# The end of a decoder step rearranged: low parts, projection, norms and gates

## Chip, cores and metric

One NeuronCore of a Trainium2 chip runs the whole program. The metric is the device time of one execution in microseconds (us). PE is TensorE, DVE VectorE, ACT ScalarE, POOL GpSimd, SP SyncE.

## What is computed

One decoder layer on 576 tokens (512 of a prompt, 64 of eight samples) with 2048 channels. The change touches what follows the expert (PEER) block:

```
x = x + peer(rms_norm(x, ln2))
x = x + sigmoid(rms_norm(x, ln_ple) @ w_ple_gate) * (p @ w_ple_proj)
y = rms_norm(x, ln_final)          # rms_norm(x,g) = x * rsqrt(mean(x*x)+eps) * g
```

## The kernel before

Activations lie feature-major in SBUF: `x` is 16 tiles (KD) of 128 channels by 576 tokens (T). Products are made in about fp32 by three matmuls of rounded operands: high times high, high times low and low times high. So each weight block of 128x1024 (512 KB) is loaded by SP (`loads`, `value_load`), rounded by ACT to `whi`, and its low part `raw - whi` is made by DVE or POOL (`split`, `value_low`; "lowering" below). There are two buffers for ordinary blocks and four in the value phase. Each engine runs its own program in order and waits on semaphores.

**Value phase** (DVE's `values`, L1530 to L1560; PE matmuls at L2085). 32 groups of 8 blocks, two output tiles a block. PE multiplies the expert activations `a_hi`, `a_lo` (416 tokens) with the value blocks; DVE adds each PSUM tile to `x`, lowers blocks, makes the next group's activations (`product` L1497, `low` L1505; ACT's `a_hi` between them), and does five `axpy` (L1530) a group for the other 160 tokens, for which POOL gathers one element (`pick`, L575) and one row of 8 KB a partition (`row`, L583) for each. Of every four value blocks POOL lowers the third (L591): blocks 2, 6, 10 and so on. PE starts group g when all four activations of the group are lowered (`a_rdy`). At the phase's start POOL does, in order: wait, lower block 2, two memsets, 10 picks, 5 rows, then rows and picks of the next groups, each row waiting for the `axpy` that frees its buffer, with block 6 lowered after two of these.

**End.** PE transposes the gathered sums (L2100, L2104) and DVE adds them to `x` (nine adds; semaphore `gx`). DVE lowers two blocks and `p` (`hi_lo`), and PE makes the 16 tiles of `p @ w_ple_proj` (2x2 K-blocks, 12 matmuls a tile, four tiles a weight block); DVE copies each to `proj` (L1594). Then `norm(2)`: ACT squares a tile, PE sums it over the channels by a matmul with ones (L1658), the two in turns for 16 tiles; DVE and ACT form the root (`rms_m`, Sqrt, reciprocal and a Newton step, L978 to L984); DVE scales, ACT rounds, DVE lowers each of 16 tiles `h`. Then 16 gate tiles, 96 matmuls each, two weight blocks each: ACT takes the sigmoid out of PSUM, DVE multiplies with `proj` and adds to `x`. Then `norm(3)`, again 16 squares and sums after the last gate, the root, 16 scalings (L1022), and 8 DMAs of `y`.

Of the kernel before, what the change touches and what calls it, by code (L numbers as in the profile page):

```python
# [19 lines left out]
F32 = mybir.dt.float32  # L20
# [6 lines left out]
P = 128  # L27
# [125 lines left out]
def build(nc, d, o):  # L153
    ctx = ExitStack()
    with ctx:
# [126 lines left out]
        def v_slot(b):  # L282
# [4 lines left out]
        (p_hi, p_lo, proj, sg), _ = run(rM, ("p_hi", [P, 2, T], F32R), ("p_lo", [P, 2, T], F32R),  # L287
                                        ("proj", [P, KD, T], F32), ("sg", [P, 2, T], F32))
        p_raw = at("p_raw", [P, 2, T], F32, rZ + 4 * TB)
# [5 lines left out]
        def ring_b(t):  # L295
# [12 lines left out]
            a_sel axpy gx_t gx""".split()  # L308
# [7 lines left out]
        def _(sp):  # L316
# [71 lines left out]
            for n in range(KD // 2):  # L388
                sp.wait_ge(S["h_done"], 3 * KD + 2 * n + 2)
                sp.dma_start(o["y"][:, 2 * n:2 * n + 2], x[:, 2 * n:2 * n + 2]).then_inc(S["out"], 16)  # L390
# [11 lines left out]
        def _(pool):  # L402
# [191 lines left out]
            for u in range(2):  # L594
                pool.wait_ge(S[f"asp{u}"], 16 * (PRE // 2))
            pool.wait_ge(s_used, B_PG)
            pool.wait_ge(S["v_hi"], 3)
# [3 lines left out]
            for n in range(2 * GR_X):  # L601
                pick(n)
            pool.wait_ge(S["relaid"], 32 * NV)
            for n in range(GR_X):
                row(n)
            for g in range(NG):
                for i in range(GR_X):
# [4 lines left out]
                    if i == 1:  # L612
                        value_low(8 * g + 6)
# [3 lines left out]
            pool.wait_ge(S["gat"], NCHUNK)  # L617
            pool.dma_start(p_raw[:], d["pT"]).then_inc(S["p"], 16)
# [3 lines left out]
        def _(act):  # L622
# [314 lines left out]
            weights(B_PG + 2, 2)  # L937
            act.wait_ge(S["v_free"], 2 * NV)
            act.wait_ge(S["gx"], 9)
            norm(2)  # L940
            with act.Fori(0, KD // 2 - 1) as i:
                for u in range(2):
                    split(B_PG + 6 + 2 * u, [(i, 4)])
                    split(B_PG + 7 + 2 * u, [(i, 4)])

                    act.wait_ge(S["pas"], i * 2 + (u + 1))
                    nc.scalar.activation(halves(sg[:, u]), ring_b(u), ACT.Sigmoid).then_inc(s_free_b, 1)
            for n in (KD - 2, KD - 1):
                if n == KD - 2:
                    split(N_BLOCKS - 2)  # L950
                    split(N_BLOCKS - 1)
                act.wait_ge(s_used, B_PG + 4 + 2 * n + 2)
                act.wait_ge(S["pas"], n + 1)
                nc.scalar.activation(halves(sg[:, n % 2]), ring_b(n), ACT.Sigmoid).then_inc(s_free_b, 1)
            act.wait_ge(S["pas"], KD + 2)
            norm(3)
# [3 lines left out]
        def _(dve):  # L960
# [572 lines left out]
            def values(g, loops=(), more=True):  # L1533
# [3 lines left out]
                turns = (0, 1, 2, 4, 5) if not more else (3, 4, 5, 6, 7) if g == 0 else (1, 2, 3, 6, 7)  # L1537
# [4 lines left out]
                for j in range(8):  # L1542
# [12 lines left out]
                    if j in turns:  # L1555
                        axpy(g, turns.index(j), loops)

# [5 lines left out]
            values(0)  # L1563
            with dve.Fori(0, (NG - 2) // 2) as i:
# [5 lines left out]

            for q in range(4):
                dve.wait_ge(S["gx_t"], q + 1)
                src = PS[:, 4 + q, :].rearrange("p (f t) -> p f t", f=4)
                for c, t0 in ((slice(64, P), NP_TOK - 64), (slice(0, 64), NP_TOK)):
                    xt = x[:, 4 * q:4 * q + 4, t0:t0 + 64]
                    v.tensor_tensor(xt, xt, src[:, :, c], ALU.add).then_inc(S["gx"], 1)
            dve.wait_ge(S["gx_t"], 5)
            xt = x[:, :, TD:TD + TX]
            v.tensor_tensor(xt, xt, PS[:, 0, :].rearrange("p (f t) -> p f t", f=KD), ALU.add).then_inc(S["gx"], 1)
            dve.wait_ge(S["gx"], 9)  # L1580
            for u in range(2):
                split(B_PG + u)

            dve.wait_ge(S["p"], 16)
            for k in range(2):
                hi_lo(p_raw[:, k], p_hi[:, k], p_lo[:, k]).then_inc(S["p_done"], 1)
            for q in range(4):
                for m in range(4):
                    if m < 3:
# [650 lines left out]
```

## Time and profile before

| | us |
|---|---|
| median of 3 runs | 5093.37 |
| lowest, highest | 5090.38, 5096.75 |
| profiled execution, its own time | 5095.67 |
| its span in the trace | 5094.1 |

| busy in the span | us | share |
|---|---|---|
| PE | 4956.0 | 97% |
| DVE | 2410.8 | 47% |
| ACT | 1284.1 | 25% |
| POOL | 1413.1 | 28% |

The granted clock over the span is 0.984 of full speed. The shares are means over very different phases. The value phase lies at 3571 to 4760 us, the end at 4760 to 5094 us; there the views by window and the timelines of the engines are to be read.

### The profile page before, as it was taken

The numbers are of one execution on the slowest core, as the hardware profiler recorded it, in microseconds if no ns is written. First come the engines' busy times: TensorE is split into PE (matmuls) and PEld (weight loads), VectorE is DVE, ScalarE is ACT, GpSimd is POOL, SyncE is SP. The second block draws the span as 40 slices with busy tenths as digits, with TensorE's granted clock in tenths as the row PEclk, the third lists the DMA queues.
The fourth block names the chain that finished last, engine by engine and source line by source line (L and its number), as shares of the span: only waits on it lengthen the run. The fifth ranks groups of instructions, "written<-read, shape, count | busy, mean of one in ns | idle before, by whom it ended". The sixth has DMA issues, their size and how long they took to land.

```text
span 5094.1 us, 86630 instructions
## 1 busy us (share of the span) xinstructions
PE 4956.0 (97%) x34109; PEld 4834.1 (95%) x34109; DVE 2410.8 (47%) x4330; ACT 1284.1 (25%) x1701; POOL 1413.1 (28%) x928
## 2 busy tenths in 40 slices
PE   8999999999998999999999999999899999999897
PEld 7999999989997999999999999999899999999797
DVE  4333442234325789122222100000799999999633
ACT  3113332123212112222222222222222222222232
POOL 1000000010000024333333344444555555555000
PEclk9999999899999999999999999999999999999999
DMA  5553345455543443244445443333888889888222
GB/s 171 156 161 115 122 149 167 132 156 167 178 122 92 147 146 106 95 162 164 159 160 179 164 147 110 106 106 132 292 308 301 309 301 309 299 303 295 89 74 78
DMA packets 505376, 882.44 MB, mean 173 GB/s; under 512 B 34016, under 2 KB 365808, under 8 KB 482432
## 3 DMA queue, kind: packets, MB, share of 16 engines
q1 hardware_dynamic: 184128, 468.24, 27.9%
q0 software_dynamic: 50784, 278.14, 14.6%
q10 hardware_dynamic: 270336, 134.25, 9.5%
q8 instruction: 92, 1.51, 0.1%
q14 instruction: 36, 0.29, 0.0%
HBM read 796.23 MB, written 220.46 MB: 200 GB/s over the span
## 4 chain that ended last, share of the span: by engine, by line
PE 82%; DVE 9%; issue 6%; ACT 1%; POOL 1%; DMA 1%; DVEq 0%; ACTq 0%; SPq 0%; POOLq 0%
PE PS L1634 65%; PE PS L2085 10%; PE PS L2057 2%; DVE v_lo L1512 2%; DVE x L1546 1%; PE PS L1658 1%; DVE acc L1530 1%; ACT w_hi L902 1%; DVE a_lo L1505 1%; DVE af L1497 1%; DVE h_lo L1002 1%; DVE w_lo L1512 0%; PE PS L1748 0%; PE PS L2003 0%; PE PS L1686 0%
## 5 line engine op out<-in xcount | busy, mean ns | idle before, releaser
L1634 PE MATMUL PS<-h_hi,w_hi 128*128 128x288 f32 x7808 | 1714.9, 301 | 50.6 <-DVE h_lo L1002 41.0
L1634 PE MATMUL PS<-h_hi,w_lo 128*128 128x288 f32 x7808 | 1681.0, 297 | 0.0
L1634 PE MATMUL PS<-h_lo,w_hi 128*128 128x288 f32 x7808 | 1679.6, 297 | 0.0
L1634 PEld LDWEIGHTS PS<-h_hi,w_hi 128*128 128x128 f32 x7808 | 1262.8, 190 | 91.3 <-issue 63.5
L1634 PEld LDWEIGHTS PS<-h_lo,w_hi 128*128 128x128 f32 x7808 | 1265.8, 190 | 0.0
L1634 PEld LDWEIGHTS PS<-h_hi,w_lo 128*128 128x128 f32 x7808 | 1265.5, 190 | 0.0
L628 ACT ACTIVATE w_hi<-w_raw 128x1024 fp32r<-128x1024 f32 x522 | 553.2, 1060 | 2326.2 <-PE PS L1634 2295.0
L537 POOL TENSOR_TENSOR w_lo<-w_raw,w_hi 128x1024 fp32r<-128x1024 f32 x254 | 619.8, 2440 | 1528.6 <-ACT w_hi L628 1528.5
L967 DVE TENSOR_TENSOR w_lo<-w_raw,w_hi 128x1024 fp32r<-128x1024 f32 x270 | 330.2, 1224 | 662.3 <-ACT w_hi L628 646.8
L2085 PE MATMUL PS<-a_hi,v_hi 128*128 128x416 f32 x1024 | 362.4, 354 | 19.2 <-POOL v_lo L591 19.1
L1472 DVE TENSOR_SCALAR oh_j<-iota,oh_cur 128x128 f32<-128x128 f32 x416 | 117.4, 282 | 542.7 <-PE PS L2057 542.5
L2085 PE MATMUL PS<-a_hi,v_lo 128*128 128x416 f32 x1024 | 362.6, 354 | 0.0
L2085 PE MATMUL PS<-a_hi,w_lo 128*128 128x416 f32 x1024 | 361.5, 353 | 0.0
L2085 PE MATMUL PS<-a_lo,v_hi 128*128 128x416 f32 x1024 | 359.0, 351 | 0.0
L2085 PE MATMUL PS<-a_hi,w_hi 128*128 128x416 f32 x1024 | 358.8, 350 | 0.0
L2085 PE MATMUL PS<-a_lo,w_hi 128*128 128x416 f32 x1024 | 357.4, 349 | 0.0
L1497 DVE TENSOR_TENSOR af<-gl,g_in 128x416 f32<-128x416 f32 x128 | 81.1, 634 | 567.8 <-DMA g_in<-gate_scr 567.8
L583 POOL DMA_INDIRECT rows<-v_rows,row_i x160 | 202.2, 1264 | 471.5 <-DVE acc L1530 443.3
L1530 DVE SCALAR_TENSOR_TENSOR acc<-rows,a_sel,acc 128x2048 f32<-128x2048 f32 x128 | 300.3, 2346 | 8.6 <-issue 8.6
L575 POOL DMA_INDIRECT a_el<-act_scr,act_i x160 | 276.1, 1726 | 48.6 <-issue 48.6
L1546 DVE TENSOR_TENSOR x<-x,PS 128x416 f32<-128x416 f32 x512 | 277.7, 580 | 18.8 <-PE PS L2085 16.1
L892 ACT ACTIVATE a_hi<-af 128x416 fp32r<-128x416 f32 x128 | 70.7, 552 | 764.9 <-DVE af L1497 647.3
(288 smaller groups left out, 5080.0 us busy)
## 6 DMA issues: line engine op xcount, KB each, us to landing
w_raw<-in_w SPq DMA_DIRECT2D x652, 512.0 KB, 3.9
v_rows<-in_w ACTq DMA_DIRECT2D x512, 256.0 KB, 3.8
v_raw<-in_w SPq DMA_DIRECT2D x128, 512.0 KB
act_scr<-gsp POOLq DMA_DIRECT2D x128, 288.0 KB, 3.6
gate_scr<-g_st POOLq DMA_DIRECT2D x13, 2048.0 KB, 8.8
gl<-act_scr SPq DMA_DIRECT2D x32, 832.0 KB
g_in<-gate_scr SPq DMA_DIRECT2D x32, 832.0 KB
spill_scr<-spill POOLq DMA_DIRECT2D x40, 288.0 KB, 4.6
```

The source lines that it names most:

```text
L537: nc.gpsimd.tensor_tensor(wlo[:, b % 2], raw[:, b % 2], whi[:, b % 2].bitcast(F32), ALU.subtract).then_inc(s_lo, 1)
L575: pool.indirect_dma_start(a_el[:, n:n + 1], None, act_flat, bass.IndirectOffsetOnAxis(ap=act_i[:, n // GR_X, n % GR_X].unsqueeze(1), axis= ...
L583: pool.indirect_dma_start(rows[:, n % GR_X], None, v_rows, bass.IndirectOffsetOnAxis(ap=row_i[:, n // GR_X, n % GR_X].unsqueeze(1), axis=0 ...
L628: nc.scalar.activation(whi[:, b % 2], raw[:, b % 2], ACT.Copy).then_inc(s_hi, 1)
L967: v.tensor_tensor(wlo[:, b % 2], raw[:, b % 2], whi[:, b % 2].bitcast(F32), ALU.subtract).then_inc(s_lo, 1)
L1472: ch.did(v.tensor_scalar(oh_j[:, n % 2, k], iota[:], cur[:, 2:3], None, ALU.is_equal))
L1497: v.tensor_tensor(af[:, c % 2].rearrange("p (b t) -> p b t", b=ND), gl[:, par, k].rearrange("p (b t) -> p b t", b=ND), g_in[:, par, :, k], ...
L1512: v.tensor_tensor(q[2], q[0], q[1].bitcast(F32), ALU.subtract).then_inc(S["v_lo"], 1)
L1530: v.scalar_tensor_tensor(dst[:], rows[:, i], a_sel[:, bass.ds(at_step(n, kl), 1)], dst[:], ALU.mult, ALU.add).then_inc(S["axpy"], 1)
L1546: v.tensor_tensor(xt, xt, PS[:, (2 * j + m) % 8, 0:TD], ALU.add).then_inc(S["v_free"], 1)
L1634: ins = mm(dst[:, a], w[:, m, at + n], xx[:, k, a * TH:(a + 1) * TH], start=first and n == 0 and r == 0, stop=last and n == len(ks) - 1 an ...
L2085: ins = mm(PS[:, f % 8, 0:TD], w[:, m, k], xx[:, par, k], start=k + r == 0, stop=k == GRP - 1 and r == 2)
```

## The change

At the start of the value phase POOL lowers block 2 before it waits for stored activations, and block 6 after 5 picks and 5 rows; the other 5 picks follow. `p` is loaded there, and DVE takes it apart, and lowers the first two projection blocks, in the last value group, whose five `axpy` are drawn together to its steps 0 to 4.

PE transposes each quarter as soon as its tiles are free, and starts the projection's first tile before `gx` is complete. ACT meanwhile rounds `x * lns` (without the root) to `h_hi`, and squares each tile; POOL adds the squares into `ss`; PE sums only this one tile over the channels (`summed`). DVE makes the low parts between its copies (`low_part`). The factor `rstd2` is multiplied in when a gate tile leaves PSUM (DVE), and ACT's sigmoid then works in SBUF. In the gate phase ACT squares each finished `x` tile and multiplies it by `lns`, and POOL adds 14 of the 16 squares. After the last gate, PE sums `ss` and the last square, and the root and 16 plain multiplications follow. Indentation is cut by eight and unchanged lines are left out in part:

```diff
@@ -284,9 +284,13 @@
     return (raw[:, q], whi[:, q], wlo[:, q]) if q < 2 else (raw2[:, q - 2], whi2[:, q - 2], wlo2[:, q - 2])
-(p_hi, p_lo, proj, sg), _ = run(rM, ("p_hi", [P, 2, T], F32R), ("p_lo", [P, 2, T], F32R),
-                                ("proj", [P, KD, T], F32), ("sg", [P, 2, T], F32))
-p_raw = at("p_raw", [P, 2, T], F32, rZ + 4 * TB)
+(proj, sg, rms2, rstd2), _ = run(rM, ("proj", [P, KD, T], F32), ("sg", [P, 2, T], F32),
+                                 ("rms2", [P, T], F32), ("rstd2", [P, T], F32))
+p_hi = at("p_hi", [P, 2, T], F32R, rZ + 4 * TB)
+assert rZ + 7 * TB <= rE
+p_raw, p_lo = at("p_raw", [P, 2, T], F32, rR), at("p_lo", [P, 2, T], F32R, rR)
+sq4 = at("sq4", [P, 4, T], F32, rZ)
+ss = at("ss", [P, T], F32, rZ + 6 * TB)
 PS = ctx.enter_context(nc.psum_tensor("PS", [P, 8, 512], F32))
 def ring_a(t):
...
@@ -386,7 +390,7 @@
     loads(B_PG + 2, N_BLOCKS, SKIP)
     for n in range(KD // 2):
-        sp.wait_ge(S["h_done"], 3 * KD + 2 * n + 2)
+        sp.wait_ge(S["yd"], 2 * n + 2)
         sp.dma_start(o["y"][:, 2 * n:2 * n + 2], x[:, 2 * n:2 * n + 2]).then_inc(S["out"], 16)
     sp.wait_ge(S["out"], 16 * (KD // 2))
@@ -591,31 +595,43 @@
         nc.gpsimd.tensor_tensor(q[2], q[0], q[1].bitcast(F32), ALU.subtract).then_inc(S["v_lop"], 1)
     pool.wait_ge(S["index"], 1)
-    for u in range(2):
-        pool.wait_ge(S[f"asp{u}"], 16 * (PRE // 2))
     pool.wait_ge(s_used, B_PG)
-    pool.wait_ge(S["v_hi"], 3)
     value_low(2)
     nc.gpsimd.memset(acc_x[:], 0.0).then_inc(S["axpy"], 1)
-    for n in range(2 * GR_X):
+    for u in range(2):
+        pool.wait_ge(S[f"asp{u}"], 16 * (PRE // 2))
+    for n in range(GR_X):
         pick(n)
+    pool.dma_start(p_raw[:], d["pT"]).then_inc(S["p"], 16)
     pool.wait_ge(S["relaid"], 32 * NV)
         row(n)
+    value_low(6)
+    for n in range(GR_X, 2 * GR_X):
+        pick(n)
     for g in range(NG):
                 pick(GR_X * (g + 2) + i)
-            if i == 1:
+            if i == 1 and g:
                 value_low(8 * g + 6)
                 value_low(8 * g + 10)
-    pool.wait_ge(S["gat"], NCHUNK)
-    pool.dma_start(p_raw[:], d["pT"]).then_inc(S["p"], 16)
+    def add_square(r, k):
+        i = (KD - 1) * (r - 2) + k
+        pool.wait_ge(S["sqd"], KD * (r - 2) + k + 1)
+        pool.wait_ge(S["ssq"], i - 1)
+        nc.gpsimd.tensor_tensor(ss[:], ss[:], sq4[:, k % 4], ALU.add).then_inc(S["ssq"], 1)
+    for k in range(1, KD):
+        add_square(2, k)
+    for k in range(1, KD - 1):
+        add_square(3, k)
 @block.scalar
@@ -934,26 +950,52 @@
         nc.scalar.activation(whi[:, u], raw[:, u], ACT.Copy).then_inc(s_hi, 1)
-    weights(B_PG + 2, 2)
-    act.wait_ge(S["v_free"], 2 * NV)
-    act.wait_ge(S["gx"], 9)
-    norm(2)
-    with act.Fori(0, KD // 2 - 1) as i:
-        for u in range(2):
-            split(B_PG + 6 + 2 * u, [(i, 4)])
-            split(B_PG + 7 + 2 * u, [(i, 4)])
-            act.wait_ge(S["pas"], i * 2 + (u + 1))
-            nc.scalar.activation(halves(sg[:, u]), ring_b(u), ACT.Sigmoid).then_inc(s_free_b, 1)
-    for n in (KD - 2, KD - 1):
-        if n == KD - 2:
-            split(N_BLOCKS - 2)
-            split(N_BLOCKS - 1)
-        act.wait_ge(s_used, B_PG + 4 + 2 * n + 2)
-        act.wait_ge(S["pas"], n + 1)
-        nc.scalar.activation(halves(sg[:, n % 2]), ring_b(n), ACT.Sigmoid).then_inc(s_free_b, 1)
-    act.wait_ge(S["pas"], KD + 2)
-    norm(3)
+    def square(r, k):
+        if k == 0:
+            if r > 2:
+                act.wait_ge(S["summed"], r - 2)
+            dst = ss[:]
+        else:
+            if r > 2 or k > 4:
+                act.wait_ge(S["ssq"], (KD - 1) * (r - 2) + max(k - 4, 0))
+            dst = sq4[:, k % 4]
+        nc.scalar.activation(dst, x[:, k], ACT.Square).then_inc(S["sqd"], 1)
+    for k in range(KD):
+        if k == 0:
+            act.wait_ge(S["gx"], 9)
+        nc.scalar.activation(h_hi[:, k], x[:, k], ACT.Copy, scale=lns[:, 2, k:k + 1]).then_inc(S["hh2"], 1)
+        square(2, k)
+        if k in (4, 8, 12, 15):
+            split(B_PG + 1 + (k + 1) // 4)
+    split(B_PG + 6)
+    split(B_PG + 7)
+    act.wait_ge(S["ms"], 3)
+    nc.scalar.activation(rstd2[:], rms2[:], ACT.Sqrt).then_inc(S["rt"], 1)
+    def sigmoid(t):
+        act.wait_ge(s_free_b, N_SPILL + NCHUNK + t + 1)
+        nc.scalar.activation(sg[:, t % 2], sg[:, t % 2], ACT.Sigmoid).then_inc(S["sgm"], 1)
+    def squared_and_weighed(t):
+        act.wait_ge(S["pas"], t + 1)
+        square(3, t)
+        act.wait_ge(S["sqd"], KD + t + 1)
+        nc.scalar.activation(x[:, t], x[:, t], ACT.Copy, scale=lns[:, 3, t:t + 1]).then_inc(S["xl"], 1)
+    for t in range(KD):
+        if 0 < t < KD - 1:
+            split(B_PG + 6 + 2 * t)
+            split(B_PG + 7 + 2 * t)
+        sigmoid(t)
+        if t == KD - 1:
+            nc.scalar.activation(tok[:], part[:], ACT.Sqrt).then_inc(S["rt"], 1)
+        else:
+            squared_and_weighed(t)
+    squared_and_weighed(KD - 1)
+    act.wait_ge(S["ms"], 4)
+    nc.scalar.activation(rstd2[:], rms2[:], ACT.Sqrt).then_inc(S["rt"], 1)
 @block.vector
@@ -1534,7 +1576,7 @@
         bl = [(r, 8 * n) for r, n in loops]
         fl = [(r, KD * n) for r, n in loops]
-        turns = (0, 1, 2, 4, 5) if not more else (3, 4, 5, 6, 7) if g == 0 else (1, 2, 3, 6, 7)
+        turns = (0, 1, 2, 3, 4) if not more else (3, 4, 5, 6, 7) if g == 0 else (1, 2, 3, 6, 7)
         if g:
@@ -1554,6 +1596,12 @@
                 axpy(g, turns.index(j), loops)
+            if not more and j >= 5:
+                if j == 5:
+                    for q in range(2):
+                        hi_lo(p_raw[:, q], p_hi[:, q], p_lo[:, q]).then_inc(S["p_done"], 1)
+                else:
+                    split(B_PG + j - 6)
     for c in range(GRP):
@@ -1561,60 +1609,85 @@
     values(0)
+    dve.wait_ge(S["p"], 16)
     with dve.Fori(0, (NG - 2) // 2) as i:
     dve.wait_ge(S["v_free"], 2 * NV)
-    for q in range(4):
+    def gathered(q):
         dve.wait_ge(S["gx_t"], q + 1)
             v.tensor_tensor(xt, xt, src[:, :, c], ALU.add).then_inc(S["gx"], 1)
+    def projected(n):
+        q, m = n // 4, n % 4
+        if m < 3:
+            dve.wait_ge(S["vt"], NV + 3 * q + m + 1)
+        else:
+            dve.wait_ge(s_used, B_PG + q + 1)
+        v.tensor_copy(halves(proj[:, n]), ring_a(n)).then_inc(s_free_a, 1)
+    def low_part(k):
+        dve.wait_ge(S["hh2"], k + 1)
+        v.scalar_tensor_tensor(h_lo[:, k], x[:, k], lns[:, 2, k:k + 1], h_hi[:, k].bitcast(F32), ALU.mult,
+                               ALU.subtract).then_inc(S["h_done"], 1)
+    def root(r):
+        dve.wait_ge(S["summed"], r - 1)
+        v.tensor_scalar(halves(rms2[:]), PS[:, 0:2, 0:TH], 1.0 / D, EPS, ALU.mult, ALU.add
+                        ).then_inc(S["ms"], 1)
+        if r == 2:
+            split(B_PG + 7)
+        dve.wait_ge(S["rt"], 3 if r == 2 else 5)
+        inverse_root(rstd2, rms2)
+    for q in range(4):
+        gathered(q)
     dve.wait_ge(S["gx_t"], 5)
     xt = x[:, :, TD:TD + TX]
-    v.tensor_tensor(xt, xt, PS[:, 0, :].rearrange("p (f t) -> p f t", f=KD), ALU.add).then_inc(S["gx"], 1)
+    v.tensor_tensor(xt, xt, PS[:, 3, :].rearrange("p (f t) -> p f t", f=KD), ALU.add).then_inc(S["gx"], 1)
     dve.wait_ge(S["gx"], 9)
-    for u in range(2):
-        split(B_PG + u)
-    dve.wait_ge(S["p"], 16)
-    for k in range(2):
-        hi_lo(p_raw[:, k], p_hi[:, k], p_lo[:, k]).then_inc(S["p_done"], 1)
-    for q in range(4):
-        for m in range(4):
-            if m < 3:
-                dve.wait_ge(S["vt"], NV + 3 * q + m + 1)
-            else:
-                dve.wait_ge(s_used, B_PG + q + 1)
-                split(B_PG + q + 2)
-            v.tensor_copy(halves(proj[:, 4 * q + m]), ring_a(m)).then_inc(s_free_a, 1)
-    dve.wait_ge(s_free_a, A_PG + KD)
-    norm(2, True)
-    dve.sem_inc(S["pas"], 2)
+    for n in range(KD):
+        projected(n)
+        if n >= 3 and n % 2 == 1:
+            low_part((n - 3) // 2)
+        if n in (5, 9, 13):
+            split(B_PG + 2 + n // 4 - 1)
+    for k in range(7, KD):
+        low_part(k)
+        if k == 10:
+            split(B_PG + 5)
+    split(B_PG + 6)
+    root(2)
     def ple(t, loops=(), more=True):
         bl, tl = [(r, 4) for r in loops], [(r, 2) for r in loops]
+        more = more and (t > 0 or loops)
         if more:
-            split(B_PG + 4 + 2 * t + 2, bl)
-            split(B_PG + 4 + 2 * t + 3, bl)
-        dve.wait_ge(s_free_b, at_step(N_SPILL + NCHUNK + t + 1, tl))
+            split(B_PG + 6 + 2 * t, bl)
+        dve.wait_ge(s_used, at_step(B_PG + 6 + 2 * t, bl))
+        v.tensor_tensor(halves(sg[:, t % 2]), ring_b(t), halves(rstd2[:]), ALU.mult).then_inc(s_free_b, 1)
+        if more:
+            split(B_PG + 7 + 2 * t, bl)
+        dve.wait_ge(S["sgm"], at_step(t + 1, tl))
         n = at_step(t, tl)
         v.tensor_tensor(x[:, n], x[:, n], proj[:, n], ALU.add).then_inc(S["pas"], 1)
+    ple(0)
     with ch.loop(KD // 2 - 1, 2) as i:
         for u in range(2):
-            ple(u, [i])
-    ple(KD - 2)
+            ple(1 + u, [i])
     ple(KD - 1, more=False)
-    dve.wait_ge(S["pas"], KD + 2)
-    norm(3, False)
+    root(3)
+    for k in range(KD):
+        dve.wait_ge(S["xl"], k + 1)
+        v.tensor_tensor(x[:, k], x[:, k], rstd2[:], ALU.mult).then_inc(S["yd"], 1)
 @block.tensor
@@ -2094,28 +2167,45 @@
     pe.wait_ge(S["axpy"], NK_G + 2)
-    pe.wait_ge(S["v_free"], 2 * NV)
     for q in range(4):
+        pe.wait_ge(S["v_free"], 2 * NV - 3 + q)
         for f in range(4):
     for f in range(KD):
-        ins = mm(PS[:, 0, f * TX:(f + 1) * TX], acc_x[:, f * P:(f + 1) * P], sel_x[:], start=True, stop=True)
+        ins = mm(PS[:, 3, f * TX:(f + 1) * TX], acc_x[:, f * P:(f + 1) * P], sel_x[:], start=True, stop=True)
     ins.then_inc(S["gx_t"], 1)
-    pe.wait_ge(S["gx"], 9)
+    def summed(src, first=True, last=True):
+        for a in range(2):
+            ins = mm(PS[:, a, 0:TH], ones[:], src[:, a * TH:(a + 1) * TH], start=first, stop=last)
+        if last:
+            ins.then_inc(S["summed"], 1)
     pe.wait_ge(S["p_done"], 2)
             pe.wait_ge(s_free_a, A_PG + 4 * q + m - 1)
+            if q == 0 and m == 1:
+                pe.wait_ge(S["gx"], 9)
             tile(ring_a(m), None, (q % 2, m, 2), p_hi, p_lo, range(2), True, True
                  ).then_inc(S["vt"] if m < 3 else s_used, 1)
-    norm(2)
-    project(ring_b, s_free_b, N_SPILL + NCHUNK, 2 * KD, B_PG + 4, KD)
-    norm(3)
+    full_tile(ring_b(0), B_PG + 4, h_hi, h_lo, h0=2 * KD)
+    pe.wait_ge(s_free_a, A_PG + KD)
+    pe.wait_ge(S["ssq"], KD - 1)
+    summed(ss[:])
+    full_tile(ring_b(1), B_PG + 6, h_hi, h_lo)
+    with pe.Fori(1, KD // 2) as i:
+        for u in range(2):
+            pe.wait_ge(s_free_b, i * 2 + (N_SPILL + NCHUNK + u - 1))
+            full_tile(ring_b(u), B_PG + 4 + 2 * u, h_hi, h_lo, [(i, 4)])
+    pe.wait_ge(S["ms"], 3)
+    pe.wait_ge(S["ssq"], 2 * KD - 3)
+    summed(ss[:], last=False)
+    pe.wait_ge(S["sqd"], 2 * KD)
+    summed(sq4[:, (KD - 1) % 4], first=False)
 # ---- launch: host side lays data out (constants below depend on shapes alone)
```

## Rows read from the trace of the kernel before

**Rows 1.** windows: busy us (instructions) of PE, PEld, DVE, ACT, POOL; clock; DMA share; GB/s

```profile
3598.00:3615.00 17.00, 0.49 (x4) 0.14 (x2) 12.71 (x11) 1.50 (x2) 10.66 (x9) 0.61 0.99 399
...
3615.00:3617.00 2.00, 2.00 (x6) 1.92 (x7) 2.00 (x2) 1.50 (x2) 0.00 (x0) 0.50 0.97 363
...
3615.00:4760.00 1145.00, 1141.90 (x6000) 1124.27 (x6000) 1079.75 (x1116) 308.38 (x370) 610.52 (x364) 1.00 0.86 298
4760.00:4771.00 11.00, 5.50 (x48) 5.39 (x48) 7.96 (x16) 0.00 (x0) 0.00 (x0) 0.75 0.16 53
4771.00:4807.00 36.00, 29.20 (x195) 28.19 (x196) 16.10 (x21) 5.39 (x6) 0.00 (x0) 0.93 0.17 58
...
4823.00:4857.00 34.00, 18.03 (x98) 14.93 (x97) 30.87 (x39) 15.66 (x22) 0.00 (x0) 0.85 0.00 0
4857.00:5051.00 194.00, 193.67 (x1440) 193.43 (x1440) 57.28 (x59) 55.07 (x57) 0.00 (x0) 0.99 0.22 76
5051.00:5094.00 43.00, 16.98 (x64) 10.92 (x64) 20.06 (x23) 13.15 (x19) 0.00 (x0) 0.79 0.27 110
```

**Rows 2.** chain that ended last, start and length in us, what ran

```profile
4760.38 1.94 PE PS L2100 x16
4762.32 3.57 PE PS L2104 x32
...
4783.16 5.07 PE PS L1634 x36
...
4856.93 193.75 PE PS L1634 x1440
5050.71 0.66 ACT sg L954
...
5053.97 17.00 PE PS L1658 x64
...
5072.57 3.77 DVE rstd L978
```

**Rows 3.** waits between 3555 and 3640 us: total, times, longest

```profile
PE PS L2085 <- POOL v_lo L591: 16.5, 1, 16.5
```

**Rows 4.** timeline of POOL (GpSimd) at the start of the value phase

```profile
3577.24 2.39 POOL L591 TENSOR_TENSOR v_lo<-v_raw,v_hi 128x1024 fp32r<-128x1024 f32 x1 [4.59 <-DMA act_scr<-gsp]
...
3596.53 0.95 POOL L583 DMA_INDIRECT rows<-v_rows,row_i  x1 [0.30 <-issue]
...
3612.51 2.35 POOL L591 TENSOR_TENSOR v_lo<-v_raw,v_hi 128x1024 fp32r<-128x1024 f32 x1
```

**Rows 5.** timeline of DVE (VectorE) in the same stretch

```profile
3602.29 2.35 DVE L1530 SCALAR_TENSOR_TENSOR acc<-rows,a_sel,acc 128x2048 f32<-128x2048 f32 x1 [8.56 <-issue]
...
3607.19 2.35 DVE L1530 SCALAR_TENSOR_TENSOR acc<-rows,a_sel,acc 128x2048 f32<-128x2048 f32 x1
```

**Rows 6.** timeline of ACT (ScalarE) in the same stretch

```profile
3592.64 1.99 ACT L902 ACTIVATE v_hi<-v_raw 128x1024 fp32r<-128x1024 f32 x2
```

**Rows 7.** timeline of POOL late in the value phase

```profile
4692.47 2.41 POOL L591 TENSOR_TENSOR v_lo<-v_raw,v_hi 128x1024 fp32r<-128x1024 f32 x1
```

**Rows 8.** timeline of DVE, late value phase and projection

```profile
4692.74 3.23 DVE L1512 TENSOR_TENSOR v_lo<-v_raw,v_hi 128x1024 fp32r<-128x1024 f32 x1
...
4714.19 1.21 DVE L1512 TENSOR_TENSOR v_lo<-v_raw,v_hi 128x1024 fp32r<-128x1024 f32 x1
...
4751.98 2.34 DVE L1530 SCALAR_TENSOR_TENSOR acc_x<-rows,a_sel,acc_x 128x2048 f32<-128x2048 f32 x1
...
4798.77 1.41 DVE L1594 COPY proj<-PS 128x576 f32<-128x576 f32 x2
```

**Rows 9.** timeline of DVE in the gate phase

```profile
4872.60 1.23 DVE L967 TENSOR_TENSOR w_lo<-w_raw,w_hi 128x1024 fp32r<-128x1024 f32 x1 [5.17 <-ACT w_hi L628]
...
4885.40 1.23 DVE L967 TENSOR_TENSOR w_lo<-w_raw,w_hi 128x1024 fp32r<-128x1024 f32 x1 [5.17 <-ACT w_hi L628]
```

**Rows 10.** timeline of ACT just before the root of norm(2)

```profile
4821.95 1.28 ACT L641 ACT_TABLE_LOAD   x1
```

More of the change, by code:

```diff
@@ L307, in build @@
             v_raw0 v_raw1 v_raw2 v_raw3 v_hi v_lo v_lop v_used v_free relaid index el0 el1 row0 row1 row2 row3 row4
-            a_sel axpy gx_t gx""".split()
+            a_sel axpy gx_t gx hh2 sqd ssq summed sgm xl yd""".split()
         S = {n: ctx.enter_context(nc.semaphore("s_" + n)) for n in names}
```

## Prediction

> **What bounds the kernel now.** I read the windows by stage first [rows 1]. In the value phase after 3615 us PE is busy 1141.9 of 1145 us at full clock, so only its start can give time: from 3598 to 3615 PE does 4 matmuls, at a clock share of 0.61. The waits say who ends that gap: one wait of 16.5 us on POOL's low part [rows 3]. The end, 4760 to 5094 us, holds 194 us of gate matmuls in which PE never rests; around them PE works 5.5 of 11, 29 of 36 and 18 of 34 us [rows 1]. So second I read the chain that ended last [rows 2], which gives the length of each serial step there, and third the timelines of DVE, ACT and POOL, for what each step costs and what an engine has queued ahead of it.
>
> **Start of the value phase.** A group is 192 matmuls, at 1141.9/6000 = 0.190 us each 36.5 us, 4.56 a block [rows 1]. PE starts at 3571.1 (four blocks before it stops in 3598), so block 6 is wanted near 3598.4. Before, POOL lowers it at 3612.5 to 3614.9 [rows 4], since two rows stand ahead of it and each waits for an axpy, of which the first starts at 3602.3 with its row [rows 5]. The rounded block is there from about 3593.7, the first half of ACT's pair [rows 6]. After the change POOL's list is block 2, two memsets, five picks (not ten), the load of `p`, five rows, block 6. It loses five of the picks that stood ahead of the first row, and block 2 no longer waits 1.5 us for the activations: 3596.5 to 3577.2 is 19.3 us of list [rows 4], less about 6.4 us for five picks (an estimate: ten picks, 2.4 of low part and two memsets of some 1.8 make up the 19.3), less 1.5, plus 0.6 for the DMA of `p`. First row at about 3589, block 6 free to be lowered at 3595, done at 3597.5, or at 3599.2 if the first axpy has the port (below). The first row took 3602.3 - 3596.5 = 5.8 us to land [rows 4, 5], so the first axpy goes at 3594.5 to 3595.
>
> What is late next: PE begins group 1 at about 3608 and needs all four of its activations. Their last low part stands on DVE behind three axpy and three steps; a step lasts 3607.2 - 3602.3 = 4.9 us [rows 5], so 3 x 4.9 plus something under one microsecond after 3594.5 gives 3610. I put the remaining wait at 3 us (0.8 for block 6, 2.2 for the activations). The DMA share is 0.99 in this stretch before [rows 1], so rows may land later than 5.8 us: the other end is a remaining wait of 12. Block 10, also on POOL behind an axpy, is wanted 9 us into group 1 and I find it 2 us early. The clock stays at 0.50 after the stall, 6 matmuls in 2 us where 10.5 fit [rows 1], about 1.3 us to win with the stall. Gain 16.5 + 1.3 - 3 = **14.8 us**, bounds 6 and 18. The new place of the second five picks costs nothing: the group that uses them comes 15 us later.
>
> **Last value group.** New there on DVE: `p` taken apart (four short ops, about 2.3 us) and two lowerings, 1.21 us each [rows 8]. DVE's last axpy ended at 4754.3 [rows 8] and PE at 4759.7, and three of DVE's adds (1.5 us) lie between: 3.9 us are free, of 4.7 wanted, and the second lowering comes after PE's last matmul, beside the transposes. So nothing is lost, or 1 us at most. Drawing the axpy to steps 0 to 4 uses rows that were requested a group earlier.
>
> **From the last value matmul to the second gate tile.** Before: 4759.65 to 4856.93, 97.3 us [rows 2]. After, in order of the path: transposes and token matmuls 1.94 + 3.57 = 5.5 us [rows 2], and PE goes on at once with the projection. It makes 36 projection matmuls in 5.07 us [rows 2], so 16 tiles of 12 take 27.0. The half clock of the old start, 0.75 and 0.93 of full speed in two windows [rows 1], goes with the pause. DVE's share in these 27 us is 16 copies of 0.70 (two take 1.41 [rows 8]), six low parts of the same size 128x576, and three lowerings: 11.3 + 4.2 + 3.4 = 18.9, so PE sets the pace. Then ten low parts remain: copy 15 and parts 6 to 10 are six ops of 0.70, 4.2 us, the lowering of the tile's second weight block 1.1, and only then PE's second half of gate tile 0, 48 matmuls at 193.75/1440 = 0.134 [rows 2], 6.4. ACT (two ops of about 0.66 a tile, and four roundings, 25 us) and POOL keep abreast of this. POOL's 15 adds are 576 columns where the low part of 1024 took 2.41 [rows 7]: 1.36 us each, 20.3 in all. The one sum over channels is four passes at 17.00/64 = 0.27, 1.1 us [rows 2]. Together 5.5 + 27.0 + 4.2 + 1.1 + 6.4 + 1.1 = 45.3.
>
> To this comes the price of POOL beside DVE. A DVE low part that began just after POOL's took 3.23 us, where one alone took 1.21; it ended 1.1 after POOL's 2.41 was over [rows 7, 8]. So an op of DVE with both sources in SBUF waits out POOL's, while a copy out of PSUM does not. In each quarter of the projection (6.8 us) three such ops wait, each up to 1.36 less the 0.70 of the copy that ran meanwhile, 2 us on top of 4.9: DVE comes to the edge of PE's pace. With one or two waits in the tail I take +3 us; bounds 0 and 8. The Trainium skill (SBUF — State Buffer, Who interferes with whom) speaks against this step: a DVE instruction with two SBUF inputs contends with a GpSimd one that reads SBUF, and the loser is blocked for the whole instruction. By that rule, the rows agree (3.23 against 1.21 us), and the PSUM copies stay free. This part: 97.3 - 48.3 = **49.0 us**, bounds 44 and 52.
>
> **Gate phase.** Before, 15 tiles in 193.75; the steady cadence is 4885.40 - 4872.60 = 12.80 us [rows 9], so 192.0 if nothing waits. New at each tile: DVE multiplies by the root at eviction, ACT squares and scales, POOL adds. ACT has then about 4.2 us a tile and DVE 5.2 of 12.8: hidden by the matmuls. Only the start can show: from the end of gate tile 0, sum 1.1, root 0.8 + 0.7, DVE's lowering 0.45 in excess, reciprocal and Newton 3.8 + 2.4, eviction 0.8, sigmoid 0.7, two ops 1.6, square and scaling 1.4, then ACT's rounding 1.1 and DVE's lowering 1.2 for tile 2: 16.0, where PE wants it at 1.1 + 12.8 = 13.9. A wait of 2.1 us; bounds 0 and 5. Cost **0.4 us** net (194.1 against 193.75).
>
> **After the last gate.** The 17.00 us of squares and sums [rows 2] become one sum of 1.1; one more DVE multiplication (0.8) stands ahead of the sigmoid. The 16 last multiplications and the output stay. Gain **15.1 us**. A table load takes 1.28 us [rows 10]; the new small Sqrt pulls it ahead, beside DVE's two ops. If the square after it needed its old table, 1.3 to 2.6 us would come back. The Trainium skill (ScalarE: Activation LUTs, Table sets) gives about 2.7 us a load; with that figure these would be 2.7 to 5.4; the trace's 1.28 decides.
>
> **Sum.** 14.8 + 49.0 - 0.4 + 15.1 = 78.5 us. The span 5094.1 becomes 5015.6, the profiled execution 5095.67 becomes 5017.2, and the median of the runs, 2.3 below that execution, 5093.37 - 78.5 = 5014.9. I say **5015**.
>
> **Rivals.**
> *The start stalls again.* The next row, activation or block 10 is as late as block 6 was. For it: DVE has work for 1079.75 of 1145 us [rows 1], so lost time is not caught up, and the queues carry 399 GB/s there. Against: the list ahead of block 6 no longer holds a row that waits. Then 12 to 15 us of the gain are gone: 5028.
> *The shared port binds the end.* Each low part and lowering waits a whole POOL add, nine in the projection and four after it, 13 x 1.36 = 18, of which PE's 8 us of slack hide some: 8 to 12 rather than 3: 5022. Against: copies lie between them.
> *All is hidden.* No port wait, no wait at gate tile 2, the whole stall gone: 3 + 2 + 3 us more: 5007.
> *Slower.* The gate tile becomes a serial loop: eviction on DVE, sigmoid, two ops, square, scaling on ACT, and only then the next weight block is rounded. Today PE covers that chain. By the steps above it is 9.6 us a tile with two table loads of 1.28, against 12.8. It binds above 12.8, and the gain of 78.5 is spent when 15 tiles lose 5.2 each, at 18.0 us; at 19 us a tile the time would be 5015 + 15 x 6.2 = 5108. It would need twice the chain: little chance. That the change does nothing would leave 5093; the removed steps are plainly on the chain [rows 2], so I give that with it.
>
> **Chances.** My forecast, 5009 to 5021, 0.52; the start stalls again 0.17; the port binds 0.14; all hidden 0.14; slower or no change 0.03. 0.2% is about what a measurement of this kernel can tell from no change, some 10 us; all cases but the last are below 5083. Faster 0.97, same 0.01, slower 0.02. The range runs from all bounds on the good side, 5003, to the stalled start with part of the port's price, 5033.
>
> **What would show it.** Right: one wait of PE on POOL's low part near 3598 of a microsecond or so, not 16.5, and a short one on the activations at group 1; no L1658 rows at the end but two sums of one tile; the last value matmul to gate tile 1's first in 46 to 52 us; 15 gate tiles in 192 to 197; from the last gate matmul to the end 28 us instead of 43.4. Wrong: PE waiting over 6 us after 3598; DVE low parts of over 2 us in most places of the projection; a gate cadence other than 12.8.

## The result and the profile after

The changed kernel takes 5028.88 us (median of 4 runs, 5016.75 to 5031.09) against 5095.06 for the kernel before (4 runs, 5090.38 to 5096.82): ratio 0.9867, 95% interval 0.9849 to 0.9884. It is 66 us faster where I forecast 78.5; the time lies in the range (5003 to 5033), 14 us above the value named. The profiled execution took 5029.01 us, its span 5027.4.

Whole times of this kernel hide a few microseconds. Code that the change doesn't touch reaches the first value matmul at 3570.95 us in the profile of before, at 3572.56 in that of the changed kernel, and at 3563 to 3580 in those of the twelve runs below. So I compare stages in the traces. The borders are rows of PE's timeline and of the chain: first value matmul, last value matmul, first matmul of gate tile 1, last gate matmul, end. A stage has a spread too: the value phase took 1180.3, 1179.4, 1177.5 and 1177.3 us in the four profiles that have the changed kernel's order there (this one, its repeat, and the runs without additions and with the gate block sooner), so a difference under 3 us in that stage tells nothing.

| us | before | forecast | after | after, second profile |
|---|---|---|---|---|
| value phase | 1188.7 | 1173.9 | 1180.3 | 1179.4 |
| to gate tile 1 | 97.3 | 48.3 | 51.3 | 50.7 |
| 15 gate tiles | 193.75 | 194.1 | 194.7 | 196.2 |
| to the end | 43.4 | 28.3 | 28.6 | 28.3 |

Together, from the first value matmul to the end: 1523.1 before, 1454.8 after, 68.3 us less. The waits of PE from 3400 to 4780 us, the first two of which answer to [rows 3] (total, times, longest):

```profile
PE PS L2158 <- DVE a_lo L1547: 5.8, 1, 5.8
PE PS L2158 <- POOL v_lo L595: 3.1, 1, 3.1
PE PS L1707 <- DVE proj L1632: 2.4, 1, 2.4
PE PS L2158 <- DVE w_lo L1554: 0.2, 1, 0.2
```

The 16.5 us are gone, but two new waits stand at the start: 5.8 us on the activations of group 1 and 3.1 on block 10. Another wait is gone, which lies far behind the window of [rows 3]: in the kernel before PE also waited 2.6 us at 4348.71 us, on block 166. There POOL had stood still for 3.66 us in which the profile shows no wait:

```profile
4340.71 2.85 POOL L583 DMA_INDIRECT rows<-v_rows,row_i  x1 [3.66 <-issue]
```

Four of the fourteen profiles have this pause, at this block: before, start alone, end alone and all gathers first. What makes it is open. So the 8.4 us that the value phase gained are not all the start's. Of DVE's 512 additions of that phase the 64th starts 165.1 us after the first value matmul before, and 159.9 and 159.4 in the two profiles of the changed kernel (157.4 and 156.9 in the other two of its order): the start gave 5 to 8 us.

Windows after (columns as in [rows 1]):

```profile
3598.00:3615.00 17.00, 11.39 (x61) 10.95 (x59) 15.31 (x17) 5.00 (x6) 15.01 (x8) 0.95 0.99 388
3616.00:3620.00 4.00, 4.00 (x13) 3.85 (x13) 4.00 (x4) 0.00 (x0) 3.69 (x2) 0.50 1.02 370
4804.00:4999.00 195.00, 192.56 (x1443) 192.26 (x1442) 75.08 (x80) 63.80 (x77) 20.02 (x14) 1.00 0.22 73
```

PE now works 11 of the 17 us in which it had stood still, but POOL is busy 15.0 of 17 and DVE 15.3. And the clock fell to 0.50 once more behind the new wait, 13 matmuls in 4 us. It fell again behind the wait of 3.1 us: 13 matmuls from 3630 to 3634 us at 0.57, where 3622 to 3626 has 23 at 1.00. The chain of the end, which answers to [rows 2] (start, length):

```profile
4752.81 1.75 PE PS L2173 x16
4754.56 3.49 PE PS L2177 x32
4758.06 9.69 PE PS L1707 x72
...
4767.77 0.76 DVE proj L1632
4768.52 1.66 DVE h_lo L1636
4770.19 2.36 DVE w_lo L1009
4772.55 0.68 DVE proj L1632
...
4790.37 12.76 PE PS L1707 x96
4803.13 0.97 PE PS L2182 x4
4804.10 12.80 PE PS L1707 x96
...
4818.04 1.24 DVE w_lo L1009
...
4819.32 179.47 PE PS L1707 x1344
...
5002.64 2.29 PE PS L2182 x4
```

PE goes from the last value matmul into the projection without a pause, both times 17.00 us of sums have become x4 rows, and where PE waited in the projection the chain runs over a lowering on DVE at twice its length (2.36 us, three times in all), behind a low part that took twice its length the first time (1.66 us). The wait at gate tile 2 is the row at 4818.04.

### The profile page after: what moved, and what is told of

Same layout as the page of the kernel before. It is cut to its first block, busy times and chain, and to the rows that moved or that the text cites. A ratio compares the mean times of both kernels' runs of the same rounds, so it can differ in the third digit from the quotient of the medians.

```text
span 5027.4 us, 86185 instructions
## 1 busy us (share of the span) xinstructions
PE 4920.6 (98%) x33993; PEld 4810.6 (96%) x33993; DVE 2405.4 (48%) x4330; ACT 1277.8 (25%) x1705; POOL 1465.2 (29%) x957
## 4 chain that ended last, share of the span: by engine, by line
PE 95%; DVE 2%; issue 1%; POOL 1%; DMA 0%; ACT 0%; DVEq 0%; ACTq 0%; POOLq 0%
PE PS L1707 66%; PE PS L2158 22%; PE PS L2130 2%; PE PS L1731 1%; POOL a_el L579 0%; DVE h_lo L1044 0%; PE PS L1821 0%; PE PS L2076 0%; PE PS L1759 0%; PE PS L1847 0%; PE PS L1964 0%; PE PS L1954 0%; POOL rows L587 0%; DVE w_lo L1009 0%; PE PS L1835 0%
## 5 line engine op out<-in xcount | busy, mean ns | idle before, releaser
L1707 PE MATMUL PS<-h_hi,w_hi 128*128 128x288 f32 x7808 | 1712.4, 301 | 38.9 <-DVE h_lo L1044 27.6
L1707 PEld LDWEIGHTS PS<-h_hi,w_hi 128*128 128x128 f32 x7808 | 1262.2, 190 | 77.2 <-issue 50.4
```

Of the source, the lines that this page charges most:

```text
L1707: ins = mm(dst[:, a], w[:, m, at + n], xx[:, k, a * TH:(a + 1) * TH], start=first and n == 0 and r == 0, stop=last and n == len(ks) - 1 an ...
```

## Experiments

**The same kernel again.**

> The changed kernel itself, to see whether its times spread over some 14 us (5016.75 to 5031.09 in four executions, where the kernel before spreads over 7) and which waits the profiled execution has. Theory P (port): near 3598 us GpSimd's gathers are each held up by VectorE instructions with two SBUF sources, so block 10 comes 3 us late, and the first axpy waits for its row, so the last activation of group 1 comes 6 us late: two waits of 9 us together in each execution of about 5029. Theory Q (queue): the DMA queues at 0.99 busy set these waits, and they differ from execution to execution by the arrival of rows, so 5017 is an execution with hardly any such wait.

Median 5026.54 (5013.84 to 5031.59) against 5096.06. Its profile has waits of 6.2 us on `a_lo` and 2.3 on POOL's `v_lo`, and a value phase of 1179.4 us: the two waits stand in each profile of this order, of 5031.6 as of 5029.0 us. The spread of the whole times is not theirs as far as the traces show; much of it lies ahead of 3571 us. None of the executions of 5014 to 5017 us was profiled. The profile of the last run below, an execution of 5010.8 us, has a hint: from gate tile 3 on its tiles take 12.48 us each instead of 12.80, at a granted clock of 1.00 in both, 4.4 us over the phase. What switches between the two paces is open.

**Each part alone.** The start alone has POOL's new order in the kernel before; the end alone has POOL's old order in the changed kernel:

```diff
-            for n in range(GR_X):
+            for n in range(2 * GR_X):
                 pick(n)
             pool.dma_start(p_raw[:], d["pT"]).then_inc(S["p"], 16)
...
-            value_low(6)
-            for n in range(GR_X, 2 * GR_X):
-                pick(n)
...
-                    if i == 1 and g:
+                    if i == 1:
                         value_low(8 * g + 6)
```

> The kernel before with only GpSimd's new order at the start of the value phase. My forecast for this part was 14.8 us; the profile of the changed kernel shows 8.5 us (1188.5 to 1180.1 us of value phase). Theory: gain 8 to 9 us (5086), waits of 5 to 6 us on a_lo and 3 on POOL's v_lo. Rival (the parts act on each other): gain of 14 or more when alone, or under 4.

> The changed kernel with GpSimd's old order at the start (ten gathers of elements, the load of p, five rows, block 6 after two more): the end alone. Theory (the parts add up): 66 - 8.5 = 58 us less than before, near 5036, with the wait of 16 to 17 us on POOL's v_lo at 3598 back. Rival (parts act on each other): less than 52 or more than 64.

By time the start alone gave nothing that can be told: 5094.15 (10 runs, 5076.66 to 5103.3) against 5096.06, ratio 0.9997 (0.9986 to 1.0009). By stage its value phase is 1182.4 us, 6.2 less than before, with waits of 5.2 on `a_lo` and of 3.0 and 2.6 on `v_lo` (the last at block 166). I had expected 8 to 9 us; the waits at the start are those expected. The end alone took 5037.35, ratio 0.9884; its value phase is 1190.2 and the rest 274.6 us against 334.5 before, so the end brings 59.9. The old wait is back, with that on block 166 (PE's waits, 3500 to 4780 us):

```profile
PE PS L2156 <- POOL v_lo L595: 21.3, 2, 18.7
```

The parts add up to within 4 us of the whole: 6.2 + 58.4 = 64.6 of 68.3, the end's 59.9 being lessened by 1.5 of a longer value phase. Both lone parts have the wait on block 166 (2.6 us), which the whole has not. What I had mis-sized most is the start.

**Why the start gave about half or less.** POOL's timeline in the changed kernel:

```profile
3590.45 1.43 POOL L587 DMA_INDIRECT rows<-v_rows,row_i  x1 [0.30 <-issue]
...
3597.00 2.41 POOL L595 TENSOR_TENSOR v_lo<-v_raw,v_hi 128x1024 fp32r<-128x1024 f32 x1
...
3600.84 2.03 POOL L579 DMA_INDIRECT a_el<-act_scr,act_i  x1 [0.30 <-issue]
...
3605.30 2.46 POOL L579 DMA_INDIRECT a_el<-act_scr,act_i  x1 [0.31 <-issue]
...
3627.43 2.35 POOL L595 TENSOR_TENSOR v_lo<-v_raw,v_hi 128x1024 fp32r<-128x1024 f32 x1
```

and DVE's:

```profile
3599.69 2.35 DVE L1572 SCALAR_TENSOR_TENSOR acc<-rows,a_sel,acc 128x2048 f32<-128x2048 f32 x1 [3.94 <-issue]
...
3614.38 0.59 DVE L1547 TENSOR_TENSOR a_lo<-af,a_hi 128x416 fp32r<-128x416 f32 x1
```

Block 6 is in time. But the first row leaves at 3590.45 and the axpy starts at 3599.69: 9.2 us, not 5.8 [rows 4, 5]. From that axpy to the low part on which PE waits it is 15.3 us, as I had summed, so that wait is the late row's. And of the gathers behind block 6, thirteen of which fill POOL from 3599.6 to 3627.4, when block 10 is lowered at last, nine take 1.8 to 3.0 us where the others take 0.95. The gather at 3600.84 ends at 3602.87, 0.8 us after the axpy beside it.

That holds for the whole phase. Of its 320 gathers of elements and rows, 157 start while an instruction of DVE with two SBUF sources runs (64 axpy, 93 lowerings), and each of the 157 ends 0.82 to 0.86 us after that instruction (in the second profile 155 of 157, the other two 1.3 us after it). The other 163 take 0.94 to 1.03 us, the 150 among them that start beside an addition with one source in PSUM too. A gather that has started when the axpy starts is not held either (3599.57, 0.97 us long). Nor do full queues do it: five gathers of 0.94 to 1.03 us stand in this window, DVE nearly idle and the DMA share 1.06:

```profile
3583.00:3590.00 7.00, 7.00 (x39) 6.94 (x38) 0.19 (x1) 1.06 (x1) 5.61 (x7) 1.00 1.06 360
```

A plain load that POOL issues is not held: in the second profile that of `p` took 0.60 us within a lowering of DVE that had begun before it (timelines of POOL and DVE):

```profile
3592.25 0.60 POOL L606 DMA_DIRECT2D p_raw<-in_pT  x1
3592.18 1.23 DVE L1554 TENSOR_TENSOR w_lo<-w_raw,w_hi 128x1024 fp32r<-128x1024 f32 x1 [6.88 <-issue]
```

Moved ahead of the rows again, these gathers ran where DVE was idle or had short work:

> The changed kernel, but all ten element gathers stand ahead of the rows, as before the change; block 6 is still lowered right after the five rows. Theory P (GpSimd's gathers are held up by VectorE's two-source instructions): gathers 6 to 10 take 0.95 us each here, where VectorE is idle, instead of 1.8 to 2.5; block 10 is lowered 5 us or more sooner relative to the first axpy and its wait goes; but the first row leaves 6.4 us later, so block 6 is about 4 us late and the wait on the activations grows from 5.8 to some 12 less that 4: in sum 2 to 4 us slower than the changed kernel. Theory Q (saturated queues): gathers 6 to 10 keep their length of about 2 us wherever they stand.

All ten took 0.94 to 1.08 us, one of them

```profile
3591.77 1.08 POOL L579 DMA_INDIRECT a_el<-act_scr,act_i  x1 [0.30 <-issue]
```

but the rows left 6.3 us later, and the value phase is 1186.8 us, 7 more than the changed kernel where I expected 2 to 4 (5030.98 in all). PE waited 3.4 us on `a_lo` and 7.1 on POOL's low parts in two, and 2.6 on block 166. The short gathers agree with theory P, though for the last of them the queues were also less full (0.66). The next run cuts DVE's instructions short under full queues:

```diff
+                w = D if g or loops else 16
-                v.scalar_tensor_tensor(dst[:], rows[:, i], ...
+                v.scalar_tensor_tensor(dst[:, 0:w], rows[:, i, 0:w], ...
```

> The changed kernel, but the five axpy of the first group work on 16 of 2048 columns (left out: the share of 160 rows in the result; all rows are still fetched). Theory P (GpSimd's gathers are held up by VectorE's instructions with two SBUF sources): the gathers that took 1.8 to 3.0 us beside an axpy of 2.35 us fall to 0.95 to 1.8, though the DMA queues stay as full. Theory Q (full queues hold the gathers up): they stay at 1.8 to 3.0 us. PE's waits are then both shorter in either case, since VectorE has 11 us less to do.

Where an axpy of 2.35 us had run, one of 0.23 runs now, with the queues at 0.99 to 1.02 busy from 3600 to 3630 us in each 10 us, and the gathers after block 6 are short:

```profile
3606.51 0.97 POOL L579 DMA_INDIRECT a_el<-act_scr,act_i  x1 [0.16 <-issue]
3607.78 0.96 POOL L579 DMA_INDIRECT a_el<-act_scr,act_i  x1 [0.30 <-issue]
3609.05 1.21 POOL L579 DMA_INDIRECT a_el<-act_scr,act_i  x1 [0.30 <-issue]
3610.57 0.96 POOL L579 DMA_INDIRECT a_el<-act_scr,act_i  x1 [0.31 <-issue]
3611.82 1.94 POOL L579 DMA_INDIRECT a_el<-act_scr,act_i  x1 [0.30 <-issue]
```

The two longer ones began beside a lowering of DVE and ended 0.8 us after it. So theory P holds for the gathers: DVE's instructions with two SBUF sources hold them up. But PE was not relieved as both theories had it: the value phase took 1182.6 us, and the two executions 5038.71 and 5034.99. PE waited 10.5 us at the start, 6.8 of them on a lowered block, because ACT waited 11.9 us for its load, which stood behind gate values:

```profile
3640.28 1.06 ACT L918 ACTIVATE w_hi<-w_raw 128x1024 fp32r<-128x1024 f32 x1 [11.87 <-DMA w_raw<-in_w]
```
```profile
g_in<-gate_scr SPq DMA_DIRECT2D x1, 832.0 KB, 23.8
```

In this run relieved engines ask for rows sooner, and the queues, already full, give no more. The last run takes the transfers of the first five rows away as well. It puts plain loads of 16 columns of `p` in their place, and this also shortens POOL's list: the five take 2.73 us together.

> The kernel with the short axpy of the run before, whose first five rows are now fetched with 16 of 2048 columns each (left out: those 160 rows again, in fetch and in sum; 5.2 MB less are moved at the start of the value phase). In the run before, VectorE was relieved and PE still lost 10.5 us, the longest wait being 6.8 us on a block whose load stood behind gate values that took 23.8 us to land. Theory T (transfers are the next bound of the start, behind VectorE's and GpSimd's lists): that wait goes, PE's waits at the start fall under 4 us, and the value phase from 1182.6 to 1171 to 1175 us. Rival (the lists alone): waits and phase stay within 2 us.

The wait on the lowered block fell from 6.8 to 1.3 us and the value phase to 1175.8, 6.8 less. That agrees with the transfers as the next bound, though POOL's shorter list may have a share that I did not separate. It stayed 1 us above what I expected, and PE's waits came to 6.2 us instead of under 4, since it waited 4.9 us on a low part of POOL's (block 14). The timelines say why: POOL stood 10.4 us before a row, waiting for the axpy that frees its buffer; that axpy stood on DVE behind a lowering for which DVE waited 6.7 us on ACT, and ACT 6.1 us on the block's load:

```profile
3617.14 1.06 ACT L918 ACTIVATE w_hi<-w_raw 128x1024 fp32r<-128x1024 f32 x1 [6.05 <-DMA w_raw<-in_w]
```

So a late load stands behind this wait as well. Time 5018.86.

**Orders that should have been better.**

> The changed kernel, but GpSimd lowers block 10 after the second of group 1's rows instead of after the fourth. Theory P: the low part is then done some 8 us sooner, PE's wait of 3.1 us on it goes, that on a_lo (5.8) stays: 3 to 4 us faster than the changed kernel. Rival: the next thing that is late (a row, a value block of the saturated DMA) takes the wait over, and the time stays within 1 us.

> The changed kernel, but GpSimd issues the load of p after block 6 and the second five gathers, behind the rows instead of ahead of them. If the load (295 KB on the same queue) is what made the first row take 9.2 us to land instead of 5.8, the first axpy starts 2 to 3 us sooner and the wait on a_lo falls from 5.8 to about 3. If other traffic makes it, only its issue of 0.9 us is won: 0 to 1 us.

> The changed kernel, but GpSimd issues the first row ahead of the first five element gathers, and the load of p last. Theory: the first axpy then waits no longer for its row (4 us in the changed kernel) and starts when VectorE reaches it; the wait of 6 us on the last activation of group 1 falls to 2 or less, and the value phase from 1179 to 1180 us to 1175 to 1177. Rival (GpSimd's list itself is behind): the same microseconds come back as a longer wait on a low part of GpSimd's (block 10 or 14), and the phase stays at 1179.

| order | PE's waits: `a_lo`, POOL's `v_lo` | value phase | median |
|---|---|---|---|
| changed kernel, second profile | 6.2, 2.3 | 1179.4 | 5026.54 |
| block 10 two rows sooner | 6.1, 2.0 | 1179.2 | 5018.14 |
| `p` loaded after the rows | 4.0, 5.7 | 1180.9 | 5029.69 |
| first row ahead of the gathers | 6.2, 3.1 | 1180.7 | 5029.93 |

The rivals were right in all three: each value phase lies in the range of the changed kernel's four (1177.3 to 1180.3 us) or within 1 us of it, and PE loses 8 to 10 us each time. With block 10 sooner the wait on POOL stands at block 14. With `p` later the first axpy waited 0.6 us for its row instead of 4, but took 3.99 us, since POOL was lowering block 6 at that moment. With the row first, DVE's small product `a_sel` took 3.10 us instead of 0.16 and ended as this lowering did, so the first axpy began 27.6 us after the first value matmul, against 27.1. The median of 5018 for the first of these would tempt one to claim 8 us; by stage it is 0.2.

These runs also say what made the row late. The load of `p` (576 KB, not the 295 of my expectation) is part of it. With it ahead of the rows the first axpy began 9.2 and 9.5 us after the first row's issue in the changed kernel, and 7.4 in the old order, which has 5.8 without it; behind the rows, at most 6.7. But the start alone, with no such load, has 8.4. The rest I put down to the fuller queues (busy 0.98 from 3590 to 3600 us, against 0.49 from 3590 to 3597 before), which no run takes by itself.

**The port in the projection.** GpSimd's additions are left out:

```diff
-                nc.gpsimd.tensor_tensor(ss[:], ss[:], sq4[:, k % 4], ALU.add).then_inc(S["ssq"], 1)
+                pool.sem_inc(S["ssq"], 1)
```

> The changed kernel without GpSimd's 29 additions of squares (left out: both sums hold one or two squares only, so the last two norms are scaled wrongly; all other work is done). Theory (shared port): VectorE's low parts and lowerings in the projection take 0.76 and 1.22 us instead of 1.4 to 1.7 and 2.4, and the last value matmul to gate tile 1's first falls from 51.3 to 47 to 48 us, 3 to 4 us in all. Rival (PE's pace and VectorE's own work set it): less than 1 us.

The last value matmul to gate tile 1's first takes 45.65 us, 5.0 to 5.6 less than with the additions (50.4 to 51.6 in the eleven profiles that have them), and close to the 45.3 that I had summed without the port. I had expected 3 to 4 us. A lowering of DVE in the projection, with the additions (second profile) and without:

```profile
4780.81 2.45 DVE L1009 TENSOR_TENSOR w_lo<-w_raw,w_hi 128x1024 fp32r<-128x1024 f32 x1
```
```profile
4771.84 1.22 DVE L1009 TENSOR_TENSOR w_lo<-w_raw,w_hi 128x1024 fp32r<-128x1024 f32 x1
```

Median 5022.3. The port costs 5 us where I had put 3; the forecast's bounds of 0 to 8 held it. The price is still well paid: 17.00 us of sums are gone.

**The wait at gate tile 2.**

```diff
+                if t == 0:
+                    split(B_PG + 8)
                 sigmoid(t)
```

(on ACT; likewise on DVE ahead of the first eviction, and not again at tile 1).

> The changed kernel, but the first weight block of gate tile 2 is rounded before the first sigmoid and lowered before the first eviction. Theory: the wait of 2.4 us of PE at gate tile 2 goes and 15 gate tiles take 192.3 us instead of 194.7. Rival (the next step in the chain, the freed PSUM buffer or the second block, is as late): under 1 us.

The chain has one row for all 15 tiles and no wait, at 12.80 us each:

```profile
4801.55 192.00 PE PS L1714 x1440
```

So the wait of 2.4 us cost 2.7 in the first profile (194.7) and 4.2 in the second (196.2). The difference is the clock: behind the wait PE made 24 matmuls in 3 us at 1.00 in one, 16 in 3 us at 0.59 in the other:

```profile
4820.00:4823.00 3.00, 3.00 (x24) 3.00 (x24) 2.49 (x3) 1.00 (x2) 0.00 (x0) 1.00 0.68 216
```
```profile
4821.00:4824.00 3.00, 3.00 (x16) 3.00 (x15) 2.87 (x4) 0.69 (x1) 0.00 (x0) 0.59 0.60 195
```

Median 5024.94.

**All together**, first row first, block 10 sooner, gate block sooner:

> The changed kernel with three edits at once: first row ahead of the gathers, block 10 lowered after the second row of group 1, and the first weight block of gate tile 2 lowered before the first eviction. Theory: value phase 1174 to 1177 us (from 1179.4), gate phase and its start 2.9 us shorter as in e7: 5 to 8 us faster than the changed kernel. Rival: value phase unchanged, only the 2.9 us.

The rival again: value phase 1181.9 us with waits of 5.9 and 3.3, gate phase 192.0. Median 5029.08, ratio 0.9877 (0.9860 to 0.9893). The gate edit is the only one of my edits for speed that shows in a stage; no version here beats the changed kernel by more than the times can tell.

## Why the prediction came out as it did

The forecast's time was 14 us too low, and by stage 10.2 of a gain of 78.5 were missing. It was right in sign and in its parts; one part was mis-sized by about half or more. Some luck is in the number: a wait of 2.6 us at which the change did not aim went away. The number landed on the rival "the start stalls again" (5028). Its mechanism is what happened, in a smaller size than its 12 to 15 us: 7 to 10 us of the start's gain are missing. The range's lower end, 5003, is no sum of the good bounds; these give 5006.5.

- **Start of the value phase, 14.8 forecast, 5.2 measured up to the 64th addition, 8.4 over the phase.** 5.2 lies under the bound of 6. The phase holds the wait on block 166 besides, which I had overlooked in the 3 us that PE is not busy after 3615 us [rows 1]. The step that failed is "what is late next". Block 6 was ready as said. The first row took 9.2 us, outside the 5.8 on which I built, though the row with the DMA share of 0.99 had warned me; and I had priced the load of `p` at its issue alone, 0.6 us. I then had PE wait 2.2 us for the activations; it was 5.8. And "I find it 2 us early" was wrong for block 10: PE waited 3.1 us. I had priced the second five gathers at nothing because the group that uses them comes 15 us later, and looked only at who needs them, not at what they delay on POOL. I moved them in thought out of DVE's idle time into its busiest, at the length they had in its idle time; the five took 9.1 us instead of 4.8. DVE's instructions hold gathers up as they and POOL's low parts hold each other up, which I had priced in the projection alone. Nor was the 1.3 us of slow clock won, since the new waits brought it back, in this profile twice. What remains open is how the 8 to 10 us of waits divide between DVE's list, the port and the transfers; shortening DVE's instructions, and with them the first two, gave the third the wait.
- **To gate tile 1, 48.3 forecast, 51.3 and 50.7 measured.** The sum of steps without the port (45.3) was met within 0.4; the port's term was 5.0 to 5.6 instead of 3. I had let a copy of 0.70 us shorten each wait. In the trace POOL's next addition was nearly always ready, so three lowerings took 2.4 us each, while the copies out of PSUM and most of the small low parts kept their 0.7 to 0.8.
- **Gate phase, 194.1 forecast, 194.7 and 196.2 measured.** The wait of 2.1 us at gate tile 2 was 2.4, at the place and by the chain named. The clock behind it was not in the sum.
- **After the last gate, gain 15.1 forecast, 14.8 measured.** No table load stood on the path. The last sum took 2.29 us instead of 1.1, at a clock of 0.61 in its window; in the run with the gate block sooner it took, at 1.00,

```profile
4997.40 1.25 PE PS L2189 x4
```

  This is no merit of that edit, since the last run, without it, has 1.25 too.

- **Last value group.** Nothing lost, as said: `p` and the two lowerings fitted before PE's last matmul or beside the transposes. From the 448th of DVE's additions to the last matmul it is 143.9 us before and after.
- **The slower rival** did not come near: the cadence of the gate tiles stayed 12.80 us in the changed kernel.

## What to carry to other kernels

When a stall is removed at the start of a phase, everything behind it is asked for sooner: price the next wait with the engines' lists and the transfer share of the stalled stretch, not with latencies measured while the others stood idle. An instruction moved past another on a queue has the price of the time it moves into. And when whole times spread by more than the effect, cut the trace at fixed instructions and compare stages; and look for the wait's new owner before calling an edit a gain.

## What the runs showed of the hardware

GpSimd's indirect DMAs are held up by VectorE's instructions with two SBUF sources. Of 320 in the value phase, the 157 that start while such an instruction runs end 0.82 to 0.86 us after it, and are up to 3.1 us long; the others take 0.94 to 1.03, at full queues too. A plain load that GpSimd issues beside the same kind of instruction takes 0.60 us. The Trainium skill (SBUF — State Buffer, Who interferes with whom) names such a block for a GpSimd instruction that reads SBUF; it infers that `tensor_tensor` leaves descriptor generation alone, and here the measurement decides otherwise for the indirect kind; for the plain kind the 0.60 us agree with it.

A pause of PE of 2.4 us at gate tile 2 was followed by half clock in one execution and not in another, worth 1.5 us. At the start of the value phase the clock fell behind pauses of 2.0 and 2.3 us and not behind those of 1.8 and 1.9; on block 166, behind the same 2.6 us, it fell in three profiles (to 0.60, 0.62 and 0.50) and not in the fourth. So the profiles of one kernel can differ by such a dip.
